# Four-tile order for the "ab" products and a later place for two centrings, in a chunked RWKV-7 layer

## The reference

```python
def step(S, inp):
    r_t, w_t, k_t, v_t, kk_t, a_t = inp
    sa = jnp.einsum('bhvk,bhk->bhv', S, kk_t)
    S = (S * w_t[:, :, None, :]
         - sa[..., None] * (kk_t * a_t)[:, :, None, :]
         + v_t[..., None] * k_t[:, :, None, :])
    y = jnp.einsum('bhvk,bhk->bhv', S, r_t)
    return S, y
```

## Time and profile before

| | |
|---|---|
| median of 3 runs | 2394.75 us (2393.91 to 2398.04) |
| the profiled execution | 2394.0 us, span 2392.2 us |
| TensorE busy | 2355.1 us, 98% of the span |
| VectorE busy | 1539.3 us, 64% |
| ScalarE busy | 1208.6 us, 51% |
| chain that ended last, by engine | PE 91%, DVE 5%, ACT 1%, issue 1%, DMA 1% |
| mean granted TensorE clock | 0.999 |

### The profile page before, as it was taken

The page is one execution under the profiler, slowest core; times in us unless marked ns, Lnnn a source line. Parts: engine busy times, 40 slices in busy tenths (PEclk is TensorE's granted clock), DMA queues, the critical chain, the costliest instruction groups (busy, mean ns, idle before and its releaser), DMA issues.

```text
span 2392.2 us, 49316 instructions
## 1 busy us (share of the span) xinstructions
PE 2355.1 (98%) x20475; PEld 2223.1 (93%) x20475; DVE 1539.3 (64%) x1899; ACT 1208.6 (51%) x1588; POOL 17.1 (1%) x36
## 2 busy tenths in 40 slices
PE   9999999989999999999999999999999999999998
PEld 9999799879998899999999999999999888999886
DVE  8588588566774455657799886656745444555445
ACT  5586463354464456754654346465545333444343
POOL 0000000000000000000000000000000000000000
PEclk9999999999999999999999999999999999999999
DMA  9355566325555654564566565655666656665664
GB/s 281 119 184 171 182 191 184 106 74 177 180 171 186 186 158 159 172 210 133 159 194 180 164 186 185 185 179 149 195 200 178 192 186 187 186 185 181 193 187 148
DMA packets 216554, 419.90 MB, mean 176 GB/s; under 512 B 17056, under 2 KB 19440, under 8 KB 215648
## 3 DMA queue, kind: packets, MB, share of 16 engines
q1 hardware_dynamic: 207520, 397.98, 54.1%
q0 software_dynamic: 2560, 10.59, 1.4%
q10 hardware_dynamic: 6288, 8.61, 1.3%
HBM read 410.84 MB, written 6.29 MB: 174 GB/s over the span
## 4 chain that ended last, share of the span: by engine, by line
PE 91%; DVE 5%; ACT 1%; issue 1%; DMA 1%; DVEq 0%; ACTq 0%
PE ps L505 28%; PE ps L506 28%; PE ps L507 28%; DVE wlo L370 1%; PE ps L725 1%; PE ps L733 1%; PE ps L639 1%; PE ps L653 1%; DMA regions<-in_a_a 1%; ACT whi L366 1%; PE ps L989 0%; DMA wraw<-in_a_w_in 0%; PE ps L750 0%; DVE act_lo L2286 0%; PE ps L1004 0%
## 5 line engine op out<-in xcount | busy, mean ns | idle before, releaser
L370 DVE TENSOR_TENSOR wlo<-wraw,whi 128x1024 fp32r<-128x1024 f32 x752 | 916.7, 1223 | 776.9 <-ACT whi L366 775.5
L366 ACT ACTIVATE whi<-wraw 128x1024 fp32r<-128x1024 f32 x752 | 793.6, 1059 | 1035.4 <-PE ps L507 1012.6
L505 PE MATMUL ps<-act_hi,whi 128*128 128x256 f32 (+2 forms) x4480 | 1274.6, 285 | 9.7 <-DVE act_lo L2286 6.9
L506 PE MATMUL ps<-act_lo,whi 128*128 128x256 f32 (+2 forms) x4480 | 1261.5, 282 | 0.0
L507 PE MATMUL ps<-act_hi,wlo 128*128 128x256 f32 (+2 forms) x4480 | 1260.1, 281 | 0.0
L505 PEld LDWEIGHTS ps<-act_hi,whi 128*128 128x128 f32 x4480 | 842.8, 188 | 16.9 <-issue 11.9
L506 PEld LDWEIGHTS ps<-act_lo,whi 128*128 128x128 f32 x4480 | 845.6, 189 | 1.0
L507 PEld LDWEIGHTS ps<-act_hi,wlo 128*128 128x128 f32 x4480 | 843.0, 188 | 0.0
L507 PE MATMUL ps<-whi,regions_r 128*128 128x512 f32 x512 | 202.3, 395 | 0.0
L506 PE MATMUL ps<-wlo,regions_r 128*128 128x512 f32 x512 | 202.2, 395 | 0.0
L505 PE MATMUL ps<-whi,regions_r 128*128 128x512 f32 x512 | 202.2, 395 | 0.0
(11 more groups left out here) (373 smaller groups left out, 1467.4 us busy)
## 6 DMA issues: line engine op xcount, KB each, us to landing
wraw<-in_a_w_in SPq DMA_DIRECT2D x128, 512.0 KB, 3.8
wraw<-in_w_up SPq DMA_DIRECT2D x128, 512.0 KB, 3.8
wraw<-in_w_down SPq DMA_DIRECT2D x128, 512.0 KB, 4.2
wraw<-in_w_in SPq DMA_DIRECT2D x112, 512.0 KB, 3.8
wraw<-in_b_w_qg SPq DMA_DIRECT2D x64, 512.0 KB, 3.8
wraw<-in_a_w_out SPq DMA_DIRECT2D x32, 512.0 KB, 3.7
wraw<-in_w_k_shared SPq DMA_DIRECT2D x32, 512.0 KB, 3.9
wraw<-in_w_v_shared SPq DMA_DIRECT2D x32, 512.0 KB, 3.6
```

Source lines behind the costliest of these rows:

```text
L366: nc.scalar.activation(whi[:, q % RING], wraw[:, q % RING], ACT.Copy).then_inc(hi_ready, 1)
L370: nc.vector.tensor_tensor(wlo[:, q % RING], wraw[:, q % RING], whi[:, q % RING].bitcast(F32), ALU.subtract).then_inc(lo_ready, 1)
L505: mm(o, hi_s, hi_m, start=first, stop=False, skip_group_check=True)
L506: mm(o, hi_s, lo_m, start=False, stop=False, skip_group_check=True)
```

## The change

The "ab" step of a chunk is one step over both halves f = 0 and 1, where it was two steps of one half each. The 32 products are the same; their order is (f 0, p 0), (f 1, p 0), (f 0, p 1), (f 1, p 1), then the next pair of tiles. For chunks 2 and 3 the step waits once for both evictions of the chunk that had these banks (`2 * c - 2`), where each half waited for its own. The centring of value groups 0 and 1 goes from VectorE's hooks 1 and 4 to hooks 14 and 15, behind the last substitution step (hook 13) and ahead of the centring of groups 2 and 3 (hook 16). Nothing is added or taken away.

```diff
@@ -290,7 +290,7 @@
         AB_AT, TAKE_AT, AB_BANK = (0, 4, 5, 7), (0, 2, 2, 3), (6, 4, 6, 4)
         for c in range(4):
-            steps_at[AB_AT[c]] = [("ab", c, 0, 0), ("ab", c, 1, 0)]
+            steps_at[AB_AT[c]] = [("ab", c, 0, 0)]
         steps_at[10] = [("gather", 0, 0, 0)]
@@ -761,11 +761,11 @@
                 if kind == "ab":
                     if c > 1:
-                        pe.wait_ge(S["ab_ready"], 2 * c - 3 + f)
+                        pe.wait_ge(S["ab_ready"], 2 * c - 2)
                     else:
                         pe.wait_ge(S["rk_taken"], 1)
                         pe.wait_ge(S["bcm_ready"], 4)
-                    into_tokens((f,), AB_BANK[c], key(Bc, c), chan(KR, 0, ts), sig=S["ab_mm"], over=1)
+                    into_tokens((0, 1), AB_BANK[c], key(Bc, c), chan(KR, 0, ts), sig=S["ab_mm"], over=1)
@@ -2039,7 +2039,7 @@
                     for n in range(4):
-                        if 8 * s + u == (1, 4, 16, 16)[n]:
+                        if 8 * s + u == (14, 15, 16, 16)[n]:
                             centre_values(n)
```

## The result

| | before | after |
|---|---|---|
| median of 11 runs | 2394.62 us | 2400.84 us (2398.61 to 2403.11) |
| ratio | | 1.0026, 95% interval 1.0018 to 1.0034 |
| span of the profiled execution | 2392.2 us | 2399.5 us |
| mean granted clock | 0.999 | 0.996 |

The changed kernel is slower, by 6.2 us in the median. The page's first part hardly moves: TensorE's busy time falls by 0.8 us of 2355.1, since four "ab" blocks that got 0.75 us shorter each and two blocks that ran at a lower clock (the gather 1.17 us longer, the first y 1.60) nearly cancel there. So the slowdown shows as idle time of TensorE, which grew by 5.2 us in front of y and 1.4 in front of the gather.

The account below looks back on a forecast made before the run. The prediction took TensorE, busy 98% of the span, as the bound, with VectorE ending last before y. +3.8 us of delay and +1.1 for the clock gave +4.9, so 2399.6 us, range 2395.5 to 2402.

Parts of the forecast that it names:

- the centrings add 5.18 us there: Before the first y: two centrings of 2.59 us each go ahead of VectorE's transposition, delaying it by 5.18 us.
- The centrings cost nothing where they stood: Around the gather: removing both centrings frees nothing beyond the 1.34 us; VectorE idles about 3.5 us longer.
- Two of four "ab" blocks count: At the gather: two chunks at 0.67 us each make it 1.34 us earlier; the others lengthen TensorE's wait to about 1.9.
- TensorE stands 5.7 us in front of y: At the first y: TensorE arrives at 388.4 and stands still until 394.1, 5.7 us.
- Its start, +3.84: Start of the first y: VectorE 5.18 us later by the centrings, 1.34 earlier by the products, +3.84 us in sum.
- The clock: +1.1 us around the new wait: Around the wait before y: the clock falls to 1.2 GHz, costing 0 to 1.7 us, taken as 1.1.
- The clock holds: Rival at the wait before y: no clock fall, so only +3.84 us, 2398.6 us; chance 0.24.
- y waits for the load: Rival at the first y: it waits for the load behind the substitution, not the transposition; 2393.4 us, chance 0.12.
- the packing takes the gain back: Rival before the gather: ScalarE's queue, not TensorE's slab, starts the packing; 2399.9 us and more, chance 0.04.
- the four tiles give nothing: Rival in the projection's "ab" products: no gain there, so centrings cost all 5.18 us; 2399.9 to 2401.6 us, chance 0.08.

Follow-up runs that it names:

- kernel 2: The kernel before with only the two centrings moved to hooks 14 and 15, products in the old order; 2402.67 us, ratio 1.0032 to the kernel before.
- kernel 1: The changed kernel with the centrings back at hooks 1 and 4, so only the four-tile order is new; 2396.34 us, ratio 1.0003 to the kernel before.
- kernel 4: The changed kernel with all four centrings moved behind the first transposition (hooks 18, 21, 24, 27); 2393.85 us, ratio 0.9994 to the kernel before.
- kernel 7: The changed kernel with all four centrings behind the first transposition and the gather one half slab later; 2392.09 us, ratio 0.9990 to the kernel before.
- kernel 6: The changed kernel with only the group 0 centring moved to hook 14, the other at its old hook 4; 2398.18 us, ratio 1.0015 to the kernel before.
- kernel 5: The changed kernel with unread constant products filling TensorE's waits, 7 before the gather, 21 before the first y; 2396.86 us, ratio 1.0011 to the kernel before.
- kernel 3: The changed kernel with unread constant products in TensorE's waits, 13 before the gather, 40 before the first y; 2404.81 us, ratio 1.0037 to the kernel before.

## Why the prediction was right

- *VectorE ends last in front of y; the centrings add 5.18 us there.* Right: +5.17 with them alone, 2.59 for one.
- *The centrings cost nothing where they stood, once the first no longer holds the packing.* Right: VectorE idles 1.09 and 5.42 us there (1.2 and 3.5 to 3.9 were written; the low clock at the gather lengthens the second, which is 3.90 in kernel 2, where the clock held at the gather).
- *Two of four "ab" blocks count, 1.34 us at the gather, and TensorE waits there instead.* Right in kind: 1.57 measured, as a block saves 0.75, the upper end given, not 0.67 (2 x 0.75 = 1.50). That this needs the centring away was in the sum without being said; kernel 1 shows it.
- *TensorE stands 5.7 us in front of y.* Right: 5.72. Its start, +3.84, was wrong: it came 5.18 late, for the next reason. That this equals the price of two centrings is chance: the 1.57 gained at the gather and the 1.5 lost there nearly cancel.
- *The clock: +1.1 us around the new wait.* Mis-sized, and incomplete. y lost 1.6 (3.61 us to the next block instead of 2.01). The windows around y withhold (0.15 + 3 x 0.50 + 0.05) x 2 = 3.4 us of full-speed work, twice what the earlier trace rows had and the repetition that the prediction had kept as a possibility; TensorE stood still through about half of it. And I priced no fall at the gather, whose wait of 1.9 us I had forecast: there it lost 1.5, the gather and the half slab behind it, which is why the substitution's first split came only 0.04 us earlier, from ab, than before, not 1.57 (it came 1.59 earlier in kernel 4, where the clock held). The terms as measured: -1.57 + 1.5 + 5.18 + 1.6 = +6.7, against the +6.76 at the recurrence, where 4 to 5 us had been written for every later stage.
- *Rivals.* "The clock holds" fell with the windows; "y waits for the load" with kernel 2, whose gather and substitution, and so the load behind it, stand where they stood before while y is 5.17 late; "the packing takes the gain back" with the gather, 1.57 earlier; "the four tiles give nothing" with the 1.09 us blocks.

By the stage the forecast of +4.9 us was 1.8 short: 1.5 for the fall at the gather, 0.5 for the price at y, less 0.2 for the tiles. The median is only 1.2 above the forecast (2400.84 against 2399.6), because the whole run grew by 6.2 and not by 6.7; no run says where the rest went, and that part of the closeness is luck. The ratio lies above the 0.2% on whose edge the forecast stood: the prediction gave slower by over 0.2% a chance of 0.46, and 0.50 to staying within it. The stated range also held the times of three rivals, so it is the rows that decide for the mechanism, not the time.

## What to carry to other kernels

Before moving work of an engine that is "only 64% busy", look for the two waits between which it has no idle time. Work put inside such a stretch here moved the wait at its end by its full length (2.59 us a centring), at a share of 64%, and work in front of a wait for another engine cost nothing (hook 4). A faster step pays only as far as the next queue that ends last; here about half of the saved time became a wait, and that half had to be filled with weights (kernel 7) before it counted. A new wait of the matrix engine can cost more than its length, since the clock may fall at it: price that at the short waits too, with a chance.

## What the hardware showed that I had not expected

- The clock fell after waits that were shorter than the longest one before, which left it alone (2.6 us). Waits of 1.9 to 2.0 us at the gather ended in a fall in two profiles (the change, kernel 6) and in none in kernel 4; 3.1 and 3.3 us ended in one each (kernels 6 and 1), 5.72 in one twice (the change, kernel 2). The 2.6 us itself tells less than it seemed to: at the same wait of the recurrence the clock fell in seven of the nine other profiles, after 2.10 to 3.00 us. In kernel 1 it fell after 2.65 us, in kernel 6 it held after 2.65 us. The wait before, the wait of the change and the window behind that:

```profile
513.27 1.16 PE L733 MATMUL ps<-M,regions 64*64 64x64 f32 x62 [2.64 <-issue]
```
```profile
521.16 1.98 PE L733 MATMUL ps<-M,regions 64*64 64x64 f32 x61 [2.37 <-issue]
```
```profile
522.00:524.00 2.00, 1.91 (x69) 1.72 (x65) 1.34 (x2) 1.97 (x6) 0.00 (x0) 0.50 0.04 8
```

Whether a short wait costs 1.5 us is thus not settled by its length, and one profile does not show how often.
- The recurrence, in whose code nothing was changed, took from 74.5 us (kernel 5) to 79.6 us (kernel 6) and 79.95 (kernel 3) between its first product and the first matmul of the next projection, 76.3 before and 78.4 after. Its waits and falls of the clock differ from profile to profile. Between kernels 5 and 6 it is the waits alone: the clock is 1.00 throughout in both, and TensorE is busy for 62.6 and 62.8 us. The first y agrees with the theory to 0.1 us in kernels 2 and 5, but the runs of one kernel spread over some 4 us. That may be why kernel 5's median lies below its +3.6; the cause was not tested.
- 64x64 products run in 17 ns a record over four tiles (1.09 us for 64) and 29 ns when consecutive ones stay in one row half (1.84): a factor of 1.7 by the order alone. The order changes two things at once, as `into_tokens` writes each half f to a bank of its own: the tiles in turn are four instead of two, and the banks two instead of one. The gather's products change the row half each time, but on two tiles and mostly in one bank, and take 31 ns (2.01 us for 64 at full clock). So the change of row half is not enough by itself; whether the tiles or the banks count was not tested.
